# Prompt attention of the even layer: bias pieces loaded without a product by the flip matrix, queries mirrored within a tile

## The reference, cut to what matters

```python
qb = qb.reshape(B, nb, Q_BLOCK, G, R, D).astype(F32) * (D ** -0.5)
s = jnp.einsum('bnqgrd,bnwgd->bnqgrw', qb, kb)
dist = n_prev * Q_BLOCK + i[:, None] - m[None, :]
mask = ((dist >= 0) & (dist <= max_dist))[None] & (kpos >= 0)[:, None, :]
bias = tab[t5_bucket(dist * dist_scale)].reshape(Q_BLOCK, W, G, R).transpose(0, 2, 3, 1)
p, lse = masked_softmax(s + bias, mask[None, :, :, None, None, :])
o = jnp.einsum('bnqgrw,bnwgd->bnqgrd', p, vb)
```

## Time and profile before

| | |
|---|---|
| median of three runs | 3360.67 us |
| the profiled execution, its own time | 3365.25 us |
| its span, first to last instruction | 3363.6 us |
| TensorE matmul, busy | 2993.3 us, 89% |
| TensorE weight load, busy | 1968.2 us, 59% |
| VectorE, busy | 1738.5 us, 52% |
| ScalarE, busy | 1004.4 us, 30% |
| mean granted TensorE clock | 0.910 |

### The profile page before, as it was taken

The page is one execution under the profiler, slowest core; times in us unless marked ns, Lnnn a source line. Parts: engine busy times, 40 slices in busy tenths (PEclk is TensorE's granted clock), DMA queues, the critical chain, the costliest instruction groups (busy, mean ns, idle before and its releaser), DMA issues. The chain is left out here.

```text
span 3363.6 us, 62223 instructions
## 1 busy us (share of the span) xinstructions
PE 2993.3 (89%) x21873; PEld 1968.2 (59%) x21873; DVE 1738.5 (52%) x4355; ACT 1004.4 (30%) x2384; POOL 604.9 (18%) x963
## 2 busy tenths in 40 slices
PE   7899996999998999997858859799979968999978
PEld 3365454899997555564635534566646645666643
DVE  3422332888884366653445556454256754555523
ACT  1000000443342466663213321100055533444311
POOL 0000001333230000002036634000011113333200
PEclk9979997999998599995769879899989988999989
DMA  4352676666562322244659954524142128999652
GB/s 168 134 183 93 233 245 168 150 155 150 148 148 53 80 76 65 63 100 118 247 175 306 309 200 159 204 84 156 47 115 65 50 77 294 365 348 352 245 215 75
DMA packets 335505, 556.48 MB, mean 165 GB/s; under 512 B 71688, under 2 KB 220240, under 8 KB 331613
## 3 DMA queue, kind: packets, MB, share of 16 engines
q1 hardware_dynamic: 252156, 343.57, 33.2%
q0 software_dynamic: 54896, 174.12, 16.5%
q10 hardware_dynamic: 28148, 34.82, 3.0%
HBM read 490.59 MB, written 118.25 MB: 181 GB/s over the span
## 5 line engine op out<-in xcount | busy, mean ns | idle before, releaser
L1357 ACT ACTIVATE cmp_xT<-PS 64x512 f32<-64x512 f32 x260 | 154.2, 593 | 716.3 <-PE PS L1446 714.8
L1478 PE MATMUL PS<-cmp_xd,cmp_w 128*128 128x256 f32 (+1 forms) x1088 | 259.2, 378 | 0.0
L1357 DVE COPY cmp_xT<-PS 64x512 f32<-64x512 f32 x260 | 179.3, 690 | 67.7 <-PE PS L1446 62.9
L1377 POOL DMA_DIRECT2D cmp_pairs<-in_cache_nsa x256 | 151.9, 601 | 311.0 <-issue 299.1
L1478 PEld LDWEIGHTS PS<-cmp_xd,cmp_w 128*128 128x128 f32 x1088 | 195.8, 194 | 20.3
L1186 DVE CUSTOM_DVE_ANT_0 pa_S<-PS,pa_tb 128x128 f32<-128x128 f32 (+3 forms) x352 | 134.5, 419 | 98.3 <-PE PS L1073 88.5
L2160 POOL DMA_DIRECT2D s_fox_kv<-in_cache_fox x256 | 138.1, 539 | 262.7 <-PE PS L2444 201.0
L1265 ACT ACTIVATE pa_S<-pa_S,pa_st 128x63 f32<-128x63 f32 (+8 forms) x288 | 155.8, 544 | 12.4 <-DVE pa_st L1209 12.3
L1446 PE MATMUL PS<-ident,cmp_pairs 128*128 128x128 f32 x1040 | 139.7, 279 | 19.0 <-DMA cmp_pairs<-in_cache_nsa 9.5
L2160 POOL DMA_DIRECT2D s_sel_kv<-in_cache_nsa x256 | 138.0, 539 | 86.9 <-issue 68.8
L2409 PE MATMUL PS<-ident,s_fox_kv 128*128 128x128 f32 x1024 | 140.4, 281 | 8.8 <-DMA s_fox_kv<-in_cache_fox 5.9
(11 more groups left out here) (511 smaller groups left out, 5770.6 us busy)
## 6 DMA issues: line engine op xcount, KB each, us to landing
s_fox_kv<-in_cache_fox POOLq DMA_DIRECT2D x256, 256.0 KB, 7.1
s_fox_kv<-in_cache_fox SPq DMA_DIRECT2D x256, 256.0 KB, 8.5
cmp_pairs<-in_cache_nsa SPq DMA_DIRECT2D x256, 128.0 KB, 4.0
cmp_pairs<-in_cache_nsa POOLq DMA_DIRECT2D x256, 128.0 KB, 4.4
s_sel_kv<-in_cache_nsa POOLq DMA_DIRECT2D x256, 128.0 KB, 5.2
s_sel_kv<-in_cache_nsa SPq DMA_DIRECT2D x256, 128.0 KB, 5.2
out_dil_sample<-in_cache_dil_w SPq DMA_DIRECT2D x8, 4088.0 KB
HE<-even_o ACTq DMA_DIRECT2D x56, 256.0 KB, 2.1
```

The source lines that it names most:

```text
L1357: last = nc.vector.tensor_copy(dst, x) if l else nc.scalar.activation(dst, x, ACT.Copy)
L1377: eng.dma_start(pairs[64 * (i % 2):64 * (i % 2) + 64, x, i // 2], pages_of[ds(pages[i], 1), :, 0:256].rearrange("x (p l) w -> (x p) l w", ...
L1478: last = nc.tensor.matmul(dst, w1[:, kv, weight, l, :], src, start=(l == 0), stop=(l == 7))
```

## The change

Bias tiles go straight from the DMA into `tb`, rows still in reverse order, and everything that is laid out by query is reversed within its tile of 128 to match:

- `raw`, the flips and their ScalarE copies are gone; preparations are 4 (with new keys) or 2. The bias load waits for `s_free` of the pair two before, as the other kinds did, and VectorE waits for the load itself in place of the preparations.
- ScalarE's copy of the queries (`prepare`, kind "q") reads each 128 columns of PSUM backwards (`back`), and so does `half_out`, so that the output comes out in the right order before `finish`.
- Maxima and sums arise in reversed order, in a new tile `ms`. A new step `sums_back` brings them to order: a product of the flip matrix and 16 columns (4 tiles, 2 heads, maximum and sum) into bank 6, and a VectorE copy from there into `o`. It stands at step 5 for the first half and at step 1 of the next pair for the second: twice in each of 14 pairs.
- The mask `same_half` is reversed in its rows.
- `bank6()` also waits for the `sums_back` copy.

```diff
--- before.py
+++ after.py
@@ -70,7 +70,7 @@
     c["causal"] = np.where(i[:, None] >= i[None], 0, NEG).astype(np.float32)
-    c["same_half"] = np.where(i[:, None] // 64 == i[None] // 64, 0, NEG).astype(np.float32)
+    c["same_half"] = np.where((127 - i[:, None]) // 64 == i[None] // 64, 0, NEG).astype(np.float32)
     c["upto"] = (i[:, None] <= i[None]).astype(np.float32)
...
@@ -845,7 +845,6 @@
         qn, kn, vn = sb("qn", [128, 2, TILES, 128]), sb("kn", [128, TILES, 128]), sb("vn", [128, 2, TILES, 128])
-        raw = sb("raw", [128, 2, 1024])
         qT, kT = sb("qT", [128, 2, SEQ]), sb("kT", [128, 2, SEQ])
...
@@ -854,12 +853,14 @@
         mq = sb("mq", [128, 2, 3])
+        ms = sb("ms", [128, 2, TILES, 2, 2])
         rd = sb("rd", [128, 4, 2])
...
             "masked", "rd_ok"))
+        flip_mm, flip_ok = sem("flip_mm"), sem("flip_ok")
         copied = [sem("copied0"), sem("copied1")]
...
@@ -885,10 +886,8 @@
         width = [128 * max(count[TILES * p:TILES * p + TILES]) for p in range(NPAIR)]
-        flips = [[(h, c, min(512, 1024 - c)) for h in range(2) for c in range(1024 - width[p], 1024, 512)]
-                 if pairs[p]["kind"] in ("rows", "halves") else [] for p in range(NPAIR)]
         preps = [[("q", 0), ("q", 1)] + ([("k", 0)] if new_kv[p] else []) + ([("k", 1)] if new_kv[p] and pairs[p]["kind"] != "cmp" else [])
-                 + [("f", x) for x in flips[p]] for p in range(NPAIR)]
+                 for p in range(NPAIR)]
         prep_at = [sum(len(x) for x in preps[:p]) for p in range(NPAIR + 1)]
...
@@ -909,6 +908,12 @@
             return [(v[r], tile[64 * r:64 * r + 64, :, :]) for r in range(2)]
+
+        turned_rows = [c["kind"] in ("rows", "halves") for c in pairs]
+
+        def back(x):
+            step = x.ap[-1][0]
+            return bass.AP(x.tensor, x.offset + 127 * step, list(x.ap[:-1]) + [[-step, 128]])
 
...
@@ -957,17 +962,15 @@
                                 sp.dma_start(t, d).then_inc(k_in, 16)
-                    if p and c["kind"] in ("rows", "halves"):
-                        sp.wait_ge(prep_ok, prep_at[p])
                     for h in range(2):
+                        if p >= 2 and h == 0:
+                            sp.wait_ge(s_free, unit_at[TILES * (p - 1)])
                         if c["kind"] in ("rows", "halves"):
...
                             v = bass.AP(v.tensor, v.offset, [[1, 128], [1, w]])
-                            sp.dma_start(raw[:, h, 0:w], v).then_inc(b_in[u], 16)
+                            sp.dma_start(tb[:, u, h, 1024 - w:1024], v).then_inc(b_in[u], 16)
                         else:
-                            if p >= 2 and h == 0:
-                                sp.wait_ge(s_free, unit_at[TILES * (p - 1)])
                             if c["kind"] == "cmp":
...
@@ -1030,12 +1033,21 @@
 
-                done = {"prep": 0, "fin": 0}
+                done = {"prep": 0, "fin": 0, "flip": 0}
 
...
                     hold(fin_ok, done["fin"])
+                    hold(flip_ok, done["flip"])
+
+                def sums_back(p, half):
+                    if turned_rows[p]:
+                        bank6()
+                        done["flip"] += 1
+                        wait(prob, 2 * (TILES * p + 4 * half + 4))
+                        nc.tensor.matmul(PS[:, PREP:PREP + 16], E.flip[:], ms[:, p % 2, 4 * half:4 * half + 4].rearrange("p n h x -> p (n h x)"),
+                                         start=True, stop=True).then_inc(flip_mm, 1)
 
...
@@ -1053,11 +1065,6 @@
                                 last = nc.tensor.transpose(PS[:, PREP + 128 * i:PREP + 128 * i + 128], kn[:, 4 * x + i, :], E.ident[:])
-                    else:
-                        h, c, w = x
-                        wait(b_in[u], 16 * 2 * (p // 2 + 1))
-                        at = c - (1024 - width[p])
-                        last = nc.tensor.matmul(PS[:, PREP:PREP + w], E.flip[:], raw[:, h, at:at + w], start=True, stop=True)
                     last.then_inc(prep_mm, 1)
...
@@ -1123,17 +1130,22 @@
                         scores(i + 3)
+                    if n == 5:
+                        sums_back(p, 0)
                     if n == 6:
...
                         values(i - 1)
+                    if p and n == 1:
+                        sums_back(p - 1, 1)
                     if p and n == 2:
...
                 values(len(steps) - 1)
+                sums_back(NPAIR - 1, 1)
                 finish(NPAIR - 1, 1)
...
@@ -1164,22 +1176,20 @@
                     if n == 0:
-                        if c["kind"] == "cmp":
-                            hold(b_in[u], 32 * (p // 2 + 1))
-                        elif c["kind"] == "fox":
+                        if c["kind"] == "fox":
                             hold(masked, 2 * p + 2)
                         else:
-                            hold(prep_ok, prep_at[p + 1])
-                            if c["kind"] == "halves":
-                                for h in range(2):
-                                    V.tensor_tensor(tb[:, u, h, 896:1024], tb[:, u, h, 896:1024], E.same_half[:], ALU.add)
-                                dve.drain()
+                            hold(b_in[u], 32 * (p // 2 + 1))
+                        if c["kind"] == "halves":
+                            for h in range(2):
+                                V.tensor_tensor(tb[:, u, h, 896:1024], tb[:, u, h, 896:1024], E.same_half[:], ALU.add)
+                            dve.drain()
                         if p >= 2:
...
                     L = length[i]
-                    m = o[:, u, n, :, HD:HD + 1]
+                    m = ms[:, u, n, :, 0:1] if turned_rows[p] else o[:, u, n, :, HD:HD + 1]
                     pieces = (unit_at[i + 1] - unit_at[i]) + (1 if c["kind"] == "fox" and L > 128 else 0)
...
@@ -1204,7 +1214,7 @@
                     if pieces > 1:
-                        V.tensor_reduce(o[:, u, n, :, HD], mq[:, :, 0:pieces], AX.X, ALU.max)
+                        V.tensor_reduce(m[:, :, 0], mq[:, :, 0:pieces], AX.X, ALU.max)
                         dve.drain()
...
@@ -1215,6 +1225,16 @@
                             V.tensor_copy(pT[0:KW[p], i % 2, 128 * x:128 * x + n], t_at(g, KW[p], 0, n)).then_inc(copied[1], 1)
+
+                flips = {"n": 0}
+
+                def sums_back(p, half):
+                    if turned_rows[p]:
+                        flips["n"] += 1
+                        hold(flip_mm, flips["n"])
+                        V.tensor_copy(o[:, p % 2, 4 * half:4 * half + 4, :, HD:HD + 2],
+                                      PS[:, PREP:PREP + 16].rearrange("p (n h x) -> p n h x", n=4, h=2)).then_inc(flip_ok, 1)
+                        dve.drain()
 
...
@@ -1244,25 +1269,22 @@
                     u = p % 2
-                    if kind == "f" and p >= 2:
-                        act.wait_ge(s_free, unit_at[TILES * (p - 1)])
-                        act.sem_inc(junk, 1)
                     act.wait_ge(prep_mm, prep_at[p] + j + 1)
                     if kind == "q":
-                        nc.scalar.activation(qT[:, u, 512 * x:512 * x + 512], PS[:, PREP:PREP + 512], ACT.Copy, scale=SCALE).then_inc(prep_ok, 1)
+                        v = PS[:, PREP:PREP + 512].rearrange("p (n q) -> p n q", n=4)
+                        nc.scalar.activation(qT[:, u, 512 * x:512 * x + 512].rearrange("p (n q) -> p n q", n=4), back(v) if turned_rows[p] else v,
+                                             ACT.Copy, scale=SCALE).then_inc(prep_ok, 1)
                     elif kind == "k":
...
                         nc.scalar.activation(kT[:, kv_of[p] % 2, 512 * x:512 * x + w], PS[:, PREP:PREP + w], ACT.Copy).then_inc(prep_ok, 1)
-                    else:
-                        h, c, w = x
-                        nc.scalar.activation(tb[:, u, h, c:c + w], PS[:, PREP:PREP + w], ACT.Copy).then_inc(prep_ok, 1)
 
...
                         x = S[:, i % 4, h, 0:length[i]]
-                        nc.scalar.activation(x, x, ACT.Exp, bias=st[:, i % 4, h:h + 1], accum_out=o[:, p % 2, n, h, HD + 1:HD + 2]).then_inc(prob, 1)
+                        nc.scalar.activation(x, x, ACT.Exp, bias=st[:, i % 4, h:h + 1],
+                                             accum_out=ms[:, p % 2, n, h, 1:2] if turned_rows[p] else o[:, p % 2, n, h, HD + 1:HD + 2]).then_inc(prob, 1)
 
...
@@ -1277,7 +1299,8 @@
                     act.wait_ge(value, 2 * p + half + 1)
-                    nc.scalar.activation(oT[:, half], PS[:, OUT:OUT + 512], ACT.Copy).then_inc(oT_ok, 1)
+                    v = PS[:, OUT:OUT + 512].rearrange("p (n q) -> p n q", n=4)
+                    nc.scalar.activation(oT[:, half].rearrange("p (n q) -> p n q", n=4), back(v) if turned_rows[p] else v, ACT.Copy).then_inc(oT_ok, 1)
 
...
```

## The result

Six runs of each kernel: 3331.61 us median for the changed one (3328.70 to 3347.12), 3359.85 us for the one before. The ratio is 0.9925, 95% interval 0.9903 to 0.9947, so 28 us less; 3334 was predicted. The profiled execution has 3330.61 us of its own time, against 3365.25 before.

A forecast was written before the change was run, and what follows sets the result against it. TensorE was taken as nearly full in the even layer's prompt attention, with VectorE limiting some steps. Pair gains of 32.4 us less 5 for bank turns gave 27: 3365.25 to 3338 profiled, median 3334, range 3317 to 3356.

The forecast's parts named there:

- TensorE's freed room, 48 us: Even layer's prompt attention: removed flips free 38.9 us of TensorE, bank waits before flips another 9.1 us.
- Where VectorE is late: Steps shrink by the flip or to VectorE's busy time plus 0.5 us; pair gains sum to 32.4 us.
- 7 us of products and 5 us of bank turns: Added on TensorE: 28 products at 0.25 us; 10 of 28 bank turns not hidden by VectorE, 0.5 us each.
- its last term: Bank turns around sums_back not hidden by VectorE: 5 us off 32.4, leaving net 27 us.
- Dilated pairs: Five dilated pairs gain about 0.6 us each from removed 256-column flips and bank waits, less added products: 3 us.
- Edits costed at nothing: ScalarE's lost copies, its 56 backwards copies at 0.597 us as forward, and the later bias load: no gain or cost counted.
- TensorE alone: Rival: VectorE's floors are too high, only TensorE's time counts; 41 us go, 3320 us; chance 12%.
- The slower case by backwards reads: Rival: ScalarE's reversed copies take longer and TensorE waits; 3384 us at 1.5 us each; chance 5%.
- The slower case by the clock: Rival: the clock falls earlier in the dilated pairs at the stage's end; up to 3378 us; chance 6%.
- The signs: Expected: TensorE busy some 35 us less, no preparation wait for VectorE, steps 1 and 2 VectorE-ended, copies 0.6, products 0.25 us.
- signs of being wrong: Stage shrinks over 40 or under 10 us, a query copy exceeds 1 us, or clock falls before the last two pairs.
- The stretch at 1170 us: Cited for the clock rival: still at the 1.2 GHz level at 1170 with TensorE busy all of 4.00 us.

The follow-up runs named there:

- the second profile of the changed kernel: The changed kernel measured and profiled again with nothing altered: 0.9931 of the time of the kernel before, stage 464.5 us.
- The moved wait: Changed kernel with VectorE's wait for the store moved from its first maxima to the first half's sums_back: 3324.57 us, 0.9895 of the kernel before.

## Why the prediction was right, point by point

**TensorE's freed room, 48 us.** Without `sums_back` the stage is 38.7 us shorter than before (492.2 - 453.5). Of the 9 us that are missing, 3.0 are in window and selection periods and some 6 in the dilated ones. Where nothing else steps in, the rooms are exact. In the second-last window pair, turn to turn, steps 1 to 5 before:

```profile
1239.84:1243.08 3.24, 3.24 (x21) 1.39 (x19) 2.42 (x9) 2.47 (x7) 0.00 (x0) 1.00 0.00 0
1243.08:1246.76 3.68, 3.63 (x31) 2.37 (x30) 2.62 (x12) 2.71 (x7) 0.00 (x0) 1.00 0.00 0
1246.76:1250.87 4.11, 4.11 (x33) 2.25 (x31) 3.65 (x14) 2.81 (x6) 0.89 (x1) 1.00 0.19 59
1250.87:1255.37 4.50, 4.16 (x39) 2.73 (x37) 2.85 (x11) 2.76 (x7) 0.00 (x0) 1.00 0.24 72
1255.37:1258.90 3.53, 3.09 (x36) 2.43 (x35) 2.12 (x9) 2.82 (x6) 0.00 (x0) 1.00 0.79 231
```

and after:

```profile
1219.73:1223.25 3.52, 3.11 (x25) 1.81 (x23) 2.52 (x10) 2.60 (x6) 0.00 (x0) 1.00 0.00 0
1223.25:1226.39 3.14, 3.14 (x28) 2.04 (x28) 2.28 (x11) 2.21 (x5) 0.00 (x0) 1.00 0.00 0
1226.39:1229.45 3.06, 3.06 (x31) 1.96 (x29) 2.38 (x9) 2.21 (x5) 0.36 (x1) 1.00 0.01 3
1229.45:1233.53 4.08, 3.74 (x36) 2.43 (x35) 3.56 (x16) 2.67 (x6) 0.53 (x1) 1.00 0.44 133
1233.53:1237.87 4.34, 3.42 (x38) 2.72 (x36) 2.92 (x14) 2.86 (x7) 0.00 (x0) 1.00 0.54 156
```

Step 3 loses 1.05 us for a wide flip of 1.06, step 4 loses 0.42 for a narrow one of 0.42. The read of rows 5 was right to the hundredth.

**Where VectorE is late: the step that failed.** The prediction gave each step a floor of VectorE's busy time plus 0.5 us. For steps 1 to 4 of this pair it forecast 3.5, 4.04, 3.24 and, by TensorE, 3.64. By its own cut, from VectorE's first copy of a step to that of the next, they took:

```profile
1220.42:1224.14 3.72, 3.31 (x26) 2.01 (x27) 2.91 (x13) 2.25 (x7) 0.00 (x0) 1.00 0.00 0
1224.14:1228.71 4.57, 4.57 (x38) 2.71 (x40) 3.53 (x14) 3.67 (x9) 0.00 (x0) 1.00 0.00 2
1228.71:1231.71 3.00, 2.66 (x29) 2.11 (x30) 2.64 (x12) 1.51 (x4) 0.89 (x1) 1.00 0.38 115
1231.71:1234.72 3.01, 2.91 (x29) 1.75 (x26) 2.65 (x13) 2.40 (x7) 0.00 (x0) 1.00 0.21 65
```

Steps 3 and 4 went below the floor of 3.24 and the 3.64, step 2 is half a microsecond above its 4.04; the sum, 14.30 us, is near the forecast's 14.42. The VectorE column of the cut by TensorE's turns, above, tells why single floors fail: over the five steps it is busy 13.66 us before and 13.66 after, but in other steps, 3.65 us in step 3 before and 2.38 after, then 3.56 in step 4. It works three steps ahead and against a queue, so such a floor could hold for a run of steps, but not for one; here the run has room (13.66 of 18.14 us). That a floor was not what held step 1 was tested (a product more costs as much there as in step 5); for the other steps it is read from these rows. What remains is 0.81 us in step 5, with the new product and TensorE standing for a VectorE copy. Window and selection periods lost 3.0 us to all of this (28.7 gained of 31.7 without `sums_back`), where the forecast's floors took some 9 with the products of `sums_back` in them.

**`sums_back`.** Its 7 us of products and 5 us of bank turns came to 11.5 us. The room of a product was 0.22 us (0.25 taken), the bank wait 0.4 (0.5 taken). But the prediction let VectorE's floors hide the price in step 1, 0.25 for the copy and no product, and it was paid in full there, 0.69 us a pair. The two errors, floors too high and this price too small, work against each other. Before its last term the forecast has 22.4 us in window and selection pairs; with the 5 us of bank turns shared out it has 17 to 20, and 21.6 were measured. The dilated pairs have 1 to 3 us in it, and -1.0 was measured. So the total of 27 owes its accuracy to luck: 2 to 4 us too little in one group and as much too much in the other.

**Dilated pairs.** Forecast 3 us, measured -1.0. The missing term is the wait for the store. It was in the trace of before as a small wait, and the prediction neither listed it nor asked what shorter pairs and a new step behind it do to it. VectorE's waiting for stores went from 6.2 us to 12.6, or to 8.3 in the second profile of the changed kernel, with the dilated periods as long; what repeats is that TensorE now stands behind it, 9.2 and 9.3 us. By steps, from turn to turn, step 6 of four dilated pairs is 8.7 us longer in all than before (3.08, 3.22, 6.00 and 5.98 us against 2.40, 2.18, 1.97 and 3.02). The moved wait gives 10.5 us back and settles this cause, with the clock's part in it not separated. In that version the dilated pairs gain 10.4 us against before, slightly over TensorE's 9.2, where the clock was also up for longer.

**Edits costed at nothing.** The backwards reads and the bias load behind `s_free` were free, the reads by their measured 594 ns. No wait of VectorE for a bias load appears.

**The rivals.** TensorE alone (41 us less) is wrong for the whole, but its mechanism is nearer for single steps of window and selection pairs than the floors were: 1.05 for 1.06 us, and 0.86 for an added product. What it leaves out is the bank turns. The slower case by backwards reads is refuted. The slower case by the clock did not come in its size: the stage's time at half clock went from 137 to 117 us, and 113 in the second profile. Its mechanism is real, though, in the dilated pairs: the clock fell next to TensorE's standing of 3.53 and 3.58 us, at 1491.0 and 1511.4. Before, it fell at 1529.1, behind the first step of the last pair but one. The first six steps of this pair, then mostly at half clock, were now at full clock and 7.0 us shorter in all, for the clock, two narrow flips and waits in the first step together. The dilated pairs' -1.0 us has this in it, beside the 8.7 us of step 6. One part of the first window period's gain (3.0 us, 1.4 forecast) is the clock's moment too: its step 0, in which the clock came up, lost 1.09 us, and 0.49 in the like pair with steady clock. Another 0.7 us is that a cmp pair leaves no `sums_back` to the pair behind it.

**The signs.** TensorE's busy time fell by 33 us (35 forecast), the copies take 0.6 us and the product 0.22. Steps 1 and 2 ended by VectorE did not come, and 3.6 us of TensorE's wait for VectorE before a preparation stayed. One of the prediction's own signs of being wrong did come: the clock fell before the last two pairs, from 1491.0 to 1494.4, at the end of the third pair from the end. The number held in spite of it.

The rule of the Trainium skill (page "TensorE: Matmul & The Clock Gate", section "Part 4: PE-mode transpose") that transposes don't count towards full clock agrees with the cmp pairs, at half clock with TensorE busy for all of 56 us; it is not separated from the effect of the narrow products there. The stretch at 1170 us that the prediction cites for it is not one of these pairs. It lies in the first step of the first window pair, and 2.08 of its 4.00 us are products with 512 columns:

```profile
1170.27 2.08 PE L1073 MATMUL PS<-pa_kT,pa_qT 64*128 64x512 f32 x4
```

The window pairs hold the 2.4 GHz level in the rows above although their steps have transposes too, so the rule alone did not decide this change.

## What to carry to other kernels

An engine that works ahead moves its work between steps, so its busy time in one step is not that step's floor: compare it with the sum of the steps that its lead covers. When a change makes pairs shorter or moves where a buffer is first written, look for the waits that guard this buffer, however small they are now, and put them at the first real write. Where a shared bank forces turns, try another order of its users; here that gave 1.65 us in each of three pairs with all flips kept. And before a gain is credited to an edit, look whether the clock changed at a place that the edit had not reached yet: over 10 of the 17 us of that run came so.

## What the runs showed of the hardware

- A negative step in ScalarE's read of PSUM costs nothing: 594 ns for 128x512, as forward.
- A float32 product with 16 columns and 128x128 weights takes 0.22 us of TensorE's room at full clock, against 0.42 with 128 and 1.06 with 512.
- TensorE can be busy for 56.00 of 56.00 us and stay at the 1.2 GHz level. During five wide products it came to the 2.4 GHz level, and lost it 6.8 us later among transposes and 63-wide products, when TensorE had been busy for 4.27 of 6.50 us.
- Behind the same 354 matmul records, the same to 0.02 us, the clock came up at 74.5 us in one execution and stayed down until 95.9 in another.
- With steady clock, window and selection periods of this stage repeat to 0.01 us between executions while the whole kernel scatters by 10 us and more. A stage cut at its own marks resolves effects that the whole time can't.
